# A second buffer for a tile's scaled rows, and VectorE's order around it, in a decoder step's first stage

## The reference, cut to what matters

```python
mod = jax.nn.silu(c) @ w_ada + b_ada
sh1, sc1, g1, sh2, sc2, g2 = [m[:, None, :] for m in jnp.split(mod, 6, axis=-1)]
h = _rmsnorm(x, n1) * (1 + sc1) + sh1
rq, rk, rv, rg, sq, sk, sv, za, zb = _split_in(h @ w_in)
...                       # retention (rq, rk, rv, rg), sliding-window attention (sq, sk, sv),
...                       # gates (za, zb), output projection, mixture of experts, final norm
```

## Time and profile before

| | |
|---|---|
| time, median of 3 runs | 1401.85 us (1398.46 to 1405.38) |
| the profiled execution's own time | 1403.35 us |
| its span, first to last instruction | 1401.5 us |
| TensorE busy, share of the span | 1233.7 us, 88% |
| VectorE busy | 750.2 us, 54% |
| ScalarE busy | 508.8 us, 36% |
| TensorE's granted clock, mean over the span | 0.95 of full |

### The profile page before, as it was taken

The page is one execution under the profiler, slowest core; times in us unless marked ns, Lnnn a source line. Parts: engine busy times, 40 slices in busy tenths (PEclk is TensorE's granted clock), DMA queues, the critical chain, the costliest instruction groups (busy, mean ns, idle before and its releaser), DMA issues.

```text
span 1401.5 us, 18007 instructions
## 1 busy us (share of the span) xinstructions
PE 1233.7 (88%) x6849; PEld 944.7 (67%) x6849; DVE 750.2 (54%) x1440; ACT 508.8 (36%) x862; POOL 175.7 (13%) x169
## 2 busy tenths in 40 slices
PE   3688989999999799999999997998299998998955
PEld 1576767667676688888888876886267666666622
DVE  0674565656656452111111115546589878888827
ACT  1442332423334221101111102111188878777732
POOL 1110000000000000000000000110122443455301
PEclk8799999999999899999999998999599999999977
DMA  9433132231420222111111005221979999999654
GB/s 355 178 134 109 37 130 84 80 120 43 146 86 20 83 99 90 45 46 45 45 45 45 0 24 204 75 75 64 342 274 375 371 347 366 345 357 372 234 212 169
DMA packets 40718, 219.75 MB, mean 157 GB/s; under 512 B 7432, under 2 KB 15056, under 8 KB 27978
## 3 DMA queue, kind: packets, MB, share of 16 engines
q1 hardware_dynamic: 32194, 197.15, 37.9%
q0 software_dynamic: 7536, 18.51, 3.9%
q10 hardware_dynamic: 928, 3.28, 0.6%
HBM read 202.03 MB, written 24.72 MB: 162 GB/s over the span
## 4 chain that ended last, share of the span: by engine, by line
PE 60%; DVE 17%; DMA 15%; issue 3%; ACT 3%; SPq 1%; POOL 0%; ACTq 0%; DVEq 0%; POOLq 0%
PE p L1893 10%; DMA G<-in_we 8%; PE p L2001 8%; PE p L1660 8%; PE p L1897 6%; PE p L1830 3%; PE psS L1893 3%; PE psS L2020 3%; PE p L1920 2%; PE psS L1920 2%; DMA M<-in_x 2%; PE psS L1897 2%; DVE work L1161 2%; PE p L1727 2%; PE p L1738 1%
## 5 line engine op out<-in xcount | busy, mean ns | idle before, releaser
L1660 PE MATMUL p<-A 128*128 128x512 f32 (+3 forms) x1080 | 262.7, 392 | 14.2 <-DVE A L1058 14.2
L1660 PEld LDWEIGHTS p<-A 128*128 128x128 f32 (+1 forms) x1080 | 178.7, 187 | 66.3 <-DVE A L1058 15.9
L2001 PE MATMUL p<-C 128*96 128x512 f32 x768 | 194.2, 405 | 22.5 <-DVE C L1545 22.5
L2001 PEld LDWEIGHTS p<-C 128*96 128x96 f32 x768 | 122.3, 165 | 79.9 <-issue 32.7
L1534 DVE TENSOR_TENSOR C<-G,C 128x2048 fp32r<-128x2048 f32 x64 | 146.1, 2284 | 38.2 <-ACT C L917 38.2
L1313 DVE TENSOR_TENSOR work<-p,work 128x344 f32<-128x344 f32 x36 | 18.6, 516 | 239.9 <-ACT work L854 239.5
L1893 PE MATMUL p<-A,B 128*128 128x344 f32 x864 | 144.5, 326 | 2.0 <-DVE M L1247 2.0
L1893 PEld LDWEIGHTS p<-A,B 128*128 128x128 f32 x864 | 138.8, 190 | 4.4 <-issue 2.2
L917 ACT CAST C<-G 128x2048 fp32r<-128x2048 f32 x64 | 122.5, 1916 | 31.5 <-DMA G<-in_we 26.4
L2020 PE MATMUL psS<-C 128*96 128x512 f32 x384 | 98.3, 406 | 5.4 <-DVE C L1557 5.4
L637 POOL DMA_INDIRECT y_dram<-M,slotY x32 | 80.3, 2509 | 103.7 <-ACT M L946 103.7
(11 more groups left out here) (286 smaller groups left out, 1808.7 us busy)
## 6 DMA issues: line engine op xcount, KB each, us to landing
G<-in_we SPq DMA_DIRECT2D x32, 2048.0 KB, 18.2
G<-in_we SPq DMA_DIRECT2D x32, 1024.0 KB, 19.0
M<-in_w_ada SPq DMA_DIRECT2D x8, 2048.0 KB, 8.1
M<-in_x SPq DMA_DIRECT2D x18, 512.0 KB, 4.0
M<-in_rope SPq DMA_DIRECT2D x45, 192.0 KB, 2.4
D<-in_w_qkv SPq DMA_DIRECT2D x4, 2048.0 KB, 7.8
F<-in_lift SPq DMA_DIRECT2D x8, 1024.0 KB, 5.0
M<-y_dram SPq DMA_DIRECT2D x8, 1024.0 KB, 12.1
```

The costliest lines, as they stand in the source:

```text
L1660: last = mm(out, x[k][:, t0:t0 + rows], y(k), start=k == 0 and j == 0, stop=k == KD - 1 and j == 2)
L2001: last = mm(up_bank[slot][0:CAP, :], x[:, k, :], kcols(w, k), start=k == 0 and j == 0, stop=k == KD - 1 and j == 2)
```

## The change

`hst` becomes a list of two buffers of the same shape, and tile t uses buffer t % 2. `h_make(t)` no longer waits for `h_rest(t-1)` but for `h_rest(t-2)`. VectorE's list becomes: `h_make(0)`; then for each t `h_make(t+1)`, `h_rest(t)`, `keys(t-1)`, `head_rest`; last `keys(8)`. The lists of the other engines stay as they are; ScalarE only reads from the tile's buffer.

```diff
-            _, D_h, _ = pieces("E", (19520, 1024, 26664), same, F32)
+            _, D_h0, _, D_h1, _ = pieces("E", (19520, 1024, 12352, 1024, 13288), same, F32)
...
-        hst = D_h[:, :].rearrange("p (k t) -> p k t", k=KD)
+        hst = [d[:, :].rearrange("p (k t) -> p k t", k=KD) for d in (D_h0, D_h1)]
...
             def h_round(t):
                 w = P if t < NT else NS
                 act.wait_ge(s["h_r"], t + 1)
-                nc.scalar.copy(hhi[:, :, t * P:t * P + w], hst[:, :, 0:w]).then_inc(s["h_hi"], 1)
+                nc.scalar.copy(hhi[:, :, t * P:t * P + w], hst[t % 2][:, :, 0:w]).then_inc(s["h_hi"], 1)
...
             def h_make(t):
-                if t:
-                    dve.wait_ge(s["h_lo"], t)
+                if t >= 2:
+                    dve.wait_ge(s["h_lo"], t - 1)
+                h = hst[t % 2]
                 for j, b in enumerate(turn_bank[t % 2]):
                     dve.wait_ge(s["hT_t"], 2 * t + j + 1)
...
-                            last = nc.vector.tensor_scalar(hst[:, kk, :], bk[:, k, :], A1T[:, kk, 0:1], B1T[:, kk, 0:1],
+                            last = nc.vector.tensor_scalar(h[:, kk, :], bk[:, k, :], A1T[:, kk, 0:1], B1T[:, kk, 0:1],
                                                            ALU.mult, ALU.add)
...
             def h_rest(t):
                 w = P if t < NT else NS
                 dve.wait_ge(s["h_hi"], t + 1)
-                nc.vector.tensor_tensor(hlo[:, :, t * P:t * P + w], hst[:, :, 0:w], hhi[:, :, t * P:t * P + w], ALU.subtract
+                nc.vector.tensor_tensor(hlo[:, :, t * P:t * P + w], hst[t % 2][:, :, 0:w], hhi[:, :, t * P:t * P + w], ALU.subtract
                                         ).then_inc(s["h_lo"], 1)
...
             dve.wait_ge(s["misc_in"], 112)
+            h_make(0)
             for t in range(NT + 1):
-                h_make(t)
-                if t >= 2:
-                    keys(t - 2)
+                if t < NT:
+                    h_make(t + 1)
                 h_rest(t)
+                if t >= 1:
+                    keys(t - 1)
                 if 4 <= t < 8:
                     head_rest(0, t - 4)
-            keys(NT - 1)
             keys(NT)
```

More of the change, by code:

```diff
@@ L1050, in h_make @@
                         ks = slice(4 * j, 4 * j + 4)
-                        link(nc.vector.tensor_tensor(hst[:, ks, 0:NS], bk[:, :, 0:NS], A1T[:, ks, 1:9], ALU.mult))
-                        last = nc.vector.tensor_tensor(hst[:, ks, 0:NS], hst[:, ks, 0:NS], B1T[:, ks, 1:9], ALU.add)
+                        link(nc.vector.tensor_tensor(h[:, ks, 0:NS], bk[:, :, 0:NS], A1T[:, ks, 1:9], ALU.mult))
+                        last = nc.vector.tensor_tensor(h[:, ks, 0:NS], h[:, ks, 0:NS], B1T[:, ks, 1:9], ALU.add)
                 last.then_inc(s["h_r"], 1)
```

## The result

The changed kernel takes 1431.47 us (median of 4 runs, 1429.44 to 1433.12) where the kernel before took 1402.72 beside it (1398.46 to 1405.38): a ratio of 1.0202, 95% interval 1.0182 to 1.0222, or 28.7 us more. The forecast was 22.6 us more, 1424, with a range to 1431. The direction and the mechanism came out as predicted. The size did not; the measured median lies half a microsecond above the range.

What follows compares the result with a forecast made beforehand. VectorE was taken to set the pace, at 5.63 us a tile. +11.2 us at full clock and +11.4 for six clock drops made +22.6, 1424 on the median; range 1411 to 1431.

Steps and rivals of the forecast that it cites:

- the wait of `h_rest` for ScalarE: On VectorE, `h_rest(t)` would find `hhi` ready and no longer wait for `h_round`; at most 3.1 us taken away.
- the ring: `kv(t-1)`, `h_turn(t+1)`, `h_make(t+1)`, `h_rest(t)`, `kv(t)` wait on one another without overlap: 7.60 us a tile, was 5.63.
- rival (c): VectorE still sets the pace and `h_rest` loses its waits for ScalarE: 3.1 us faster, 1398.7; chance 0.05.
- the start of `kv(1)`: First products behind `h_turn(2)` on TensorE: start at 60.11 against 57.73, +2.4 us.
- `kv(0)`'s delay: `kv(0)` starts 1.4 us later, at no cost because `h_turn(2)` waits for `normed(2)` until 55.54 anyway.
- the drop: TensorE's clock goes to 1.2 GHz after each of six idle gaps ahead of `kv(1)` to `kv(6)`: +11.4 us.
- rival (a): Tiles slow to 7.60 us but TensorE's clock stays up: +11.2 us, 1413; chance 0.20.
- the table's landing: The rotation table lands behind two 2 MB loads; it moves with the loop, as does TensorE's 4.69 us idle.
- rival (b): Table's landing does not move, freeing TensorE's 4.69 us idle: 1419.7 with clock drops, 1408.4 without; chance 0.07.
- The price of one: Cost of one clock drop ahead of a `kv`: between 1.55 and 2.26 us, taken as 1.9.
- that leg: Behind `kv(7)`, up to the first rotated tile: `weights(1)` goes out up to 0.65 us sooner, -0.6.
- that rule: Every burst of products behind a long wait runs cold: six at 2.26 us, 13.6 in place of 11.4, so 1426.6.

Runs made afterwards that it cites:

- the ring cut: Changed kernel with TensorE's transposes of tile t+1 ahead of `kv(t-1)` and ScalarE's `normed` one tile further ahead: 1401.05 us; `h_turn(2)` to `kv(7)` 33.70.
- one buffer as well (35.33): Kernel before, one buffer and VectorE's old order, with transposes and `normed` moved ahead: 1402.98 us; `h_turn(2)` to `kv(7)` 35.33.
- the filler run: Changed kernel plus 20 unused products of 256 columns on TensorE behind the transposes of tiles 2 to 7: 1413.31 us.
- the kernel before with the table ahead: Kernel before with only the rotation table's load issued on SyncE ahead of the two 2 MB loads: 1401.18 us, ratio 0.9991.

## Why the prediction was right on the mechanism and wrong on the size

- Right: the wait of `h_rest` for ScalarE goes, and it was worth little. With the ring cut the stretch is 2.65 us shorter, and 1.0 of that comes with one buffer as well (35.33), so some 1.6 us of one execution each are left for that wait; the prediction's bound was 3.1.
- Right: the ring. Measured at full clock in the filler run it is 7.55 us a tile (7.60 predicted), so VectorE does not set the pace and rival (c) is out; the start of `kv(1)` is later by 2.4 us as worked out; `kv(0)`'s delay was hidden by the rows' load.
- Right: the drop comes in each of the six gaps of 3.5 us, and the filler run, in which the clock stays up, took 1413.31, where rival (a) was priced at 1413.
- Right: the table's landing moves with the loop, and about 1 us of the 29 is swallowed there, not the whole idle (rival (b)): ahead of the first rotated tile it was 4.69 us and is 3.73.
- Wrong: "The price of one lies between" 1.55 and 2.26, and "I take the middle, 1.9". Measured, a tile with the drop takes 10.28 us against the ring's 7.60: 2.7 us, above the upper bound. The step that failed is this term of the sum, the price of one drop. All six bursts were low from end to end, where the row of 79.83 had been low for a part only. And the upper bound was itself too low. It was read from the row of 57.73, a tile with no turning of the keys between the products and the next transposes, and it stops where those transposes begin. The turning of the keys (0.41 against 0.27) and the first transposes run at the same low clock: from tile 2 on `kv` to the next transposes is 5.49 where 3.03 was taken, and from there to `h_make` 0.94 to 1.13 where 0.74 was. Six times 0.8 us are 4.7 of the 6.1 us missing.
- Wrong, smaller: the seventh burst. `kv(7)` follows a gap of 1.79 us and took 4.56, 1.5 us more than the full-clock 3.09; the sum had no drop there, only the range. That turns the forecast -0.6 of that leg into +0.7, as SyncE's issues in the kernel after show:

```profile
120.79 0.33 SPq L388 DMA_DIRECT2D D<-in_w_qkv  x1
126.29 0.33 SPq L391 DMA_DIRECT2D M<-in_w_ada  x1
```

  `weights(1)` goes out 2.04 us behind the start of `kv(7)`, where it was 2.94: 0.9 us sooner, where 0.6 was forecast. But `ada_weights(0)`, which waits for the products, goes out 7.54 us behind it where it was 5.97, and the table lands behind both.
- Not settled: 1.5 us of the profiled difference lie behind the stage and -1.0 ahead of it, less than the scatter between runs of one kernel.

The Trainium skill's rule cited in the prediction ("TensorE: Matmul & The Clock Gate", section "Loop structure matters more than you think"), by which every burst behind a long wait runs cold, was the better guide here: the trace agrees, with six bursts of 5.49 us out of six. The page's example is a wait for a DMA; here the wait was for other engines. Priced from the rows, that rule gave 1426.6, still below the measured time. The other rule of the Trainium skill, from "Trainium Kernel Development and Optimization", section "Best Practices", is to double-buffer so that DMA overlaps with compute. No run here tests that, for `hst` holds no transfer: the prediction took it for overlap between engines, and there the buffers alone gave 1404.12 and the order that uses them 1431.47.

## What to carry to other kernels

Before an engine's list is reordered to look one tile ahead, write down for each operand moved forward where its producer stands in the other engine's list; two lists that are each in order can close a ring that neither shows. When one engine is sent ahead through a second buffer, send its producers ahead too: here, with VectorE's list as in the change, the whole loss went only when TensorE's transposes and ScalarE's rows ran one tile further ahead as well. When a change opens regular gaps on TensorE, price the products, and everything else that TensorE does behind the gap, at the low clock in full.

## What the runs showed of the hardware

The loop settled into a steady rhythm in which the clock was low in every burst, although TensorE worked for over 6 us of each 10.28: 3.50 us of idle, 5.49 us at 1.2 GHz, the full clock back during the transposes and lost again before the next burst. Twenty products nobody needs, 2.60 us a tile, kept the granted clock at 1.00 and took 18 us off the program.

The length of a gap did not decide alone. Gaps of 1.14 to 1.16 us (filler run) never cost the clock, and those of 2.87 us and more ahead of key and value products always did. In between, the profiled executions of these kernels have eleven gaps of 1.79 to 2.22 us ahead of a `kv` of 24 products: six were followed by a slow burst (4.2 to 4.6 us), five by one of 3.1. In the kernel before with the table ahead, 1.94 us cost nothing and the next gap, 1.93 us, cost 1.5.
